# A float32 decoder trunk on one core: where three small pieces of work stand at the ends of its two mixers

## What is computed

```python
def reference(x, ffn_w_gate, ffn_w_up, ffn_w_down, norm_gain, ...):
    for i in range(DEPTH):                       # DEPTH = 2
        g = norm_gain[i]
        h = swiglu(rmsnorm(x, g[0]), ffn_w_gate[i, 0], ffn_w_up[i, 0], ffn_w_down[i, 0])
        x = x + MACARON_WEIGHT * rmsnorm(h, g[1])
        h = rmsnorm(x, g[2])
        j = i // N_MIXERS
        if i % N_MIXERS == 0:
            h = gla_mixer(h, gla_w_in[j], ..., gla_w_out[j])
        else:
            h = ssd_mixer(h, ssd_w_in[j], ..., ssd_w_out[j])
        x = x + rmsnorm(h, g[3])
        h = swiglu(rmsnorm(x, g[4]), ffn_w_gate[i, 1], ffn_w_up[i, 1], ffn_w_down[i, 1])
        x = x + MACARON_WEIGHT * rmsnorm(h, g[5])
    return x

def swiglu(h, w_gate, w_up, w_down):
    return (jax.nn.silu(h @ w_gate) * (h @ w_up)) @ w_down
```

## Time and profile before

| What | us |
|---|---|
| median of 3 runs | 1087.08 (1086.83 to 1087.44) |
| the profiled execution | 1086.96 |
| its span | 1085.2 |
| PE busy | 1075.1 |
| DVE busy | 787.6 |
| ACT busy | 652.8 |
| POOL busy | 87.2 |

### The profile page before, as it was taken

The page is one execution under the profiler, slowest core; times in us unless marked ns, Lnnn a source line. Parts: engine busy times, 40 slices in busy tenths (PEclk is TensorE's granted clock), DMA queues, the critical chain, the costliest instruction groups (busy, mean ns, idle before and its releaser), DMA issues.

```text
span 1085.2 us, 17549 instructions
## 1 busy us (share of the span) xinstructions
PE 1075.1 (99%) x6399; PEld 940.1 (87%) x6399; DVE 787.6 (73%) x1122; ACT 652.8 (60%) x1002; POOL 87.2 (8%) x138
## 2 busy tenths in 40 slices
PE   9999999999999999999999999999999999999997
PEld 7888888899888888888888888899999988888886
DVE  5867667785677666667766767889888888776664
ACT  7645446784676445458454447697777797454453
POOL 3000000011010000000000000153222211000000
PEclk9999999999999999999999999999999999999999
DMA  9864655375357555474655554595555536655531
GB/s 283 296 230 156 206 180 145 107 241 183 121 163 245 193 190 197 155 233 140 232 192 193 177 171 121 173 289 184 187 155 155 170 121 213 238 171 195 196 112 40
DMA packets 162881, 199.30 MB, mean 184 GB/s; under 512 B 6372, under 2 KB 145856, under 8 KB 162832
## 3 DMA queue, kind: packets, MB, share of 16 engines
q1 hardware_dynamic: 160288, 190.86, 53.9%
q0 software_dynamic: 2384, 7.72, 2.1%
q10 hardware_dynamic: 160, 0.08, 0.0%
HBM read 197.56 MB, written 1.08 MB: 183 GB/s over the span
## 4 chain that ended last, share of the span: by engine, by line
PE 92%; ACT 3%; DMA 2%; DVE 2%; issue 1%; SPq 0%; POOL 0%; DVEq 0%; ACTq 0%; POOLq 0%
PE ps L1772 27%; PE ps L1934 24%; PE ps L1948 13%; PE ps L1826 9%; PE ps L1835 6%; PE ps L1738 5%; PE ps L1859 4%; DMA raw<-in_ffn_w_up 1%; PE ps L1798 1%; PE ps L2294 1%; PE ps L2153 0%; ACT exps L882 0%; PE ps L2298 0%; DVE xres L1179 0%; PE ps L1757 0%
## 5 line engine op out<-in xcount | busy, mean ns | idle before, releaser
L1224 DVE TENSOR_TENSOR ws<-raw,ws 128x1024 fp32r<-128x1024 f32 x180 | 213.3, 1222 | 139.7 <-ACT ws L685 139.7
L1772 PE MATMUL ps<-ws,hT 128*128 128x512 f32 x1320 | 314.0, 392 | 0.0
L685 ACT ACTIVATE ws<-raw 128x1024 fp32r<-128x1024 f32 x183 | 184.7, 1053 | 173.2 <-PE ps L1948 160.3
L1772 PEld LDWEIGHTS ps<-ws,hT 128*128 128x128 f32 x1320 | 243.7, 188 | 49.5 <-issue 1.1
L1934 PE MATMUL ps<-xT,ws 128*128 128x512 f32 x1152 | 267.3, 389 | 0.2 <-ACT ws L685 0.2
L1934 PEld LDWEIGHTS ps<-xT,ws 128*128 128x128 f32 x1152 | 216.1, 188 | 45.5 <-ACT ws L685 0.6
L1146 DVE TENSOR_TENSOR ws<-raw,ws 128x2048 fp32r<-128x2048 f32 (+1 forms) x88 | 197.2, 2243 | 27.8 <-ACT ws L599 27.8
L599 ACT ACTIVATE ws<-raw 128x2048 fp32r<-128x2048 f32 x83 | 157.6, 1909 | 2.6 <-PE ps L1772 2.6
L1948 PEld LDWEIGHTS ps<-xT,ws 128*128 128x128 f32 x1152 | 142.6, 192 | 2.5
L1948 PE MATMUL ps<-xT,ws 128*128 128x256 f32 x1152 | 144.1, 283 | 0.0
L1826 PE MATMUL ps<-xT,ws 128*128 128x256 f32 x960 | 119.2, 284 | 0.0
(11 more groups left out here) (263 smaller groups left out, 864.3 us busy)
## 6 DMA issues: line engine op xcount, KB each, us to landing
raw<-in_ffn_w_down SPq DMA_DIRECT2D x88, 512.0 KB, 4.8
raw<-in_ffn_w_gate SPq DMA_DIRECT2D x86, 512.0 KB, 4.0
raw<-in_ffn_w_up SPq DMA_DIRECT2D x86, 512.0 KB, 5.0
raw<-in_ssd_w_in SPq DMA_DIRECT2D x48, 512.0 KB, 4.7
raw<-in_gla_w_in SPq DMA_DIRECT2D x24, 512.0 KB, 4.8
raw<-in_ssd_w_out SPq DMA_DIRECT2D x16, 512.0 KB, 4.3
raw<-in_gla_w_out SPq DMA_DIRECT2D x8, 512.0 KB, 5.5
exps<-cs_rows POOLq DMA_DIRECT2D x8, 512.0 KB, 5.1
```

Of the source, the lines that this page charges most:

```text
L685: act.activation(ws[:, 0:2, 0, c], raw[:, 0:2, c], ACT.Copy).then_inc(gu_hi, 1)
L1224: dve.tensor_tensor(ws[:, 0:2, 1, c], raw[:, 0:2, c], ws[:, 0:2, 0, c].bitcast(F32), ALU.subtract).then_inc(gu_lo, 1)
L1772: mm = pe.matmul(ps[:, 2 * t + n, :], hT[:, par, j, a, t * P:(t + 1) * P], ws[:, slot, b, off:off + 512], start=(first and j + a + b == 0) ...
```

## The change

Three edits.

1. In the SSD mixer's body `ahead` DVE writes the whole low part of the output weights of group n-2 (128x2048) at once, ahead of `norm`, where before it wrote the first half. The second half, which stood in the body `tail` between `wm` and the copy of the state, is gone from there.
2. At the ends of both mixers each of POOL's two low parts of 128x2x512 elements is made by four instructions of 128x2x128. The semaphore is still raised once for each 128x2x512.
3. At the boundary behind both mixers ACT writes the high parts of blocks 0 and 1 of x's first 128 tokens ahead of the last `post_square` (t = 1, second half), and the other six behind it.

```diff
@@ -554,9 +554,12 @@
                     pool.wait_ge(gu_hi, unit * NQ + NQ)
                     pool.wait_ge(x_ready, 4 * (b - 1) + 2)
                     pool.wait_ge(gu_lo, unit * NQ + NQ - 2)
-                    for c in (slice((NQ - 2) * QW, (NQ - 1) * QW), slice((NQ - 1) * QW, NQ * QW)):
-                        pool.tensor_tensor(ws[:, 0:2, 1, c], raw[:, 0:2, c], ws[:, 0:2, 0, c].bitcast(F32),
-                                           op=ALU.subtract).then_inc(gu_lo, 1)
+                    for q in range(NQ - 2, NQ):
+                        for o in range(0, QW, QW // 4):
+                            c = slice(q * QW + o, q * QW + o + QW // 4)
+                            ins = pool.tensor_tensor(ws[:, 0:2, 1, c], raw[:, 0:2, c], ws[:, 0:2, 0, c].bitcast(F32),
+                                                     op=ALU.subtract)
+                        ins.then_inc(gu_lo, 1)
                 if b > 0:
                     pool.wait_ge(post_read, 4 * b)
                     pool.dma_start(gpost[:, :], gain_row(2 * b + 1)).then_inc(gpost_in, 16)
@@ -756,9 +759,10 @@
                 post_square(b, 1, 0)
                 after_mixer = b < NPH and PHASES[b - 1][0] != "ffn"
                 if after_mixer:
+                    x_high(b, 0, range(2))
                     post_square(b, 1, 1)
                 if b < NPH:
-                    x_high(b, 0, range(KD // 2))
+                    x_high(b, 0, range(2 if after_mixer else 0, KD // 2))
                 if not after_mixer:
                     post_square(b, 1, 1)
                     post_root(b, 1)
@@ -1605,8 +1609,6 @@
                                 lo(SLOT_P3, g + n0[SLOT_P3])
                                 x_convolved(state_copied)
                             else:
-                                if tail:
-                                    lo_half(*out_unit(n - 2, n, n0), 1)
                                 state_copied()
                             if tail:
                                 transposed(C)
@@ -1682,7 +1684,7 @@
                     if first and ssd:
                         norm(g, tail)
                     if ssd and ahead:
-                        lo_half(*out_unit(g - 1, n, n0), 0)
+                        lo(*out_unit(g - 1, n, n0))
                     if ssd and tail:
                         lo_half(*out_unit(n - 1, n, n0), 0)
                     if scan and not (first and ssd) and not second:
```

## The result

| What | before | changed |
|---|---|---|
| median of 22 runs, us | 1087.08 (1086.80 to 1087.57) | 1088.45 (1088.09 to 1089.58) |
| span of the profiled execution | 1085.2 | 1086.8 |
| DVE busy, us and instructions | 787.6, 1122 | 789.2, 1121 |
| POOL busy, us and instructions | 87.2, 138 | 89.5, 150 |

The changed kernel takes 1.0013 times the time of before (95% interval 1.0007 to 1.0019): 1.37 us more, a small difference that is clear of the noise, and inside the 0.2% that the prediction calls no change. The forecast was 1087.6, in a range of 1086.1 to 1088.6.

What follows compares the result with a forecast made beforehand. The prediction took PE's row of matmuls (92% of the chain) to bound the kernel. Its terms, +0.4 for edit 1, +0.1 behind GLA and 0 behind SSD, made +0.5 us on 1087.08, so 1087.6, range 1086.1 to 1088.6.

Steps and rivals of the forecast that it cites:

- the ceiling: PE's waits at the mixers' ends, together 1.7 us or 0.16% of the time: the most the change could bring.
- the list of rivals: Its no-queue case at the SSD norm: one-input L1523 and L1528 pass POOL; total -0.2 us, 1086.9, chance 0.30.
- the case with one held step: SSD mixer's norm, edit 1: POOL holds one of L1529 to L1531; L1542 +0.35, saved 0.32 cancelled, 0 or -0.1.
- A quarter of 256 elements should take 0.62 to 0.66, like L525: POOL's low parts at both mixers' ends: eight quarters take 5.0 to 5.2 for 4.75, POOL ending 0.3 to 0.4 later.
- the rival of costly quarters: Both boundaries: quarters of 0.72 or more hold both x-update halves, 0.6 a boundary; total +1.7, 1088.8, chance 0.15.
- The bookkeeping of holds: DVE at both boundaries: L1151 waits for one POOL quarter, L1152 for the next, so L1151's saving is spent.
- may find POOL idle: DVE's L1179 at both boundaries: starts 308.67 and 899.06 before, POOL's last quarter ending at 308.8 and 899.1.
- So the 0.26 that PE gains behind GLA is lost 5 us later: Edit 3: PE's earlier first high part is offset by the later x update; +0.1 behind GLA, 0 behind SSD.
- the prediction's own sign: Check in the changed profile: forecast wrong if a POOL quarter takes over 0.7, or L1529 to L1531 take 0.16 each.

Runs made afterwards that it cites:

- edits 1 and 3 freed of their holds: Edits 1 and 3, POOL's last two dx products after `wm`, one-input Newton steps at t = 1 behind both mixers, against the kernel before: 1085.96 against 1086.93.
- dx later: Edit 1 alone with POOL's last two side products (dx, L525) issued only after DVE's `wm`, against the kernel before: 1086.72 against 1086.98, ratio 0.9999.

## Why the prediction came out as it did

- **What bounds the kernel, and the ceiling.** Right: PE carries the chain before and after, no kernel left the 0.2%, and the one with the lowest median, edits 1 and 3 freed of their holds, gains 0.97 of the 1.7 us that the prediction gave as the ceiling.
- **Edit 1**, forecast +0.4, measured +0.28 in the changed kernel and +0.31 alone. Each step came as worked out: L517 at 2.53, three steps held, and, counted from L517's start, L1542 0.86 later (4.73 for 3.87; forecast 0.9), L2294 0.86 later (6.60 for 5.74) and L2298, free of its wait, 0.48 later (7.69 for 7.21; forecast 0.5 to 0.6). Of these 0.48 PE had 0.20 back by its transposes behind SSD, a little more than the prediction allowed. What it didn't name is where PE first waits for the held steps: 0.56 at the transposes of y. Two details were wrong without harm to the sum. L1523 didn't pass POOL freely, as the list of rivals has it (see below). And the case with one held step was priced at +0.35 for L1542 and 0 or -0.1 for PE, as if none had been held before; but L1530 had been. With one held step and dx later, L1542 came 0.11 later (3.98 for 3.87) and PE gained 0.34.
- **Edit 2: the mis-sized term.** The step that failed is "A quarter of 256 elements should take 0.62 to 0.66, like L525": it took 0.742, eight took 5.62 in place of 5.0 to 5.2, and POOL ended 0.87 later than before in place of 0.3 to 0.4. L525 wasn't a like row: it has the same count but other operands, and no fp32r output. The like row was L558 itself, but one size of it can't show a fixed part. Rows 4 had a hint of one, though: 512 elements took 1.04 in one instruction (L520) and 1.20 in two (L525), 0.16 for one more instruction. Six more at that price, an estimate from these rows, make 4.75 + 0.96 = 5.71, close to the 5.62. The prediction had set 0.7 as the mark above which its forecast is wrong, and 0.72 for the rival of costly quarters, and the boundaries went that rival's way: +0.66 and +0.42 where the forecast had +0.1 and 0 and the rival about 0.6 on top of each. The bookkeeping of holds was half right. Both Newton steps took a hold, as in the forecast, but of both halves of the x update only one was held, behind SSD; behind GLA the update waited for POOL's last end instead.
- **The x update** "may find POOL idle": so it was behind GLA (309.45 against POOL's end at 309.40). Counted from POOL's start it still came 0.68 later than before (5.67 for 4.99), since POOL's end was 0.87 later, less the 0.19 by which L1179 had followed that end before.
- **Edit 3.** "So the 0.26 that PE gains behind GLA is lost 5 us later" is right for the edit alone (+0.02), by the hold that ends with POOL. With quarters it cost a further 0.27 behind GLA, which the prediction, with its quarters at a lower price, did not have. PE started its 22 matmuls there without a wait, as forecast.
- **Sum.** The time, 1088.45, lies 0.85 above the forecast and inside the range. The range held because it took in most of the costly quarters, to which 0.15 was given. So the number came out inside the range with the boundaries mis-sized, nearer to the rival's 1088.8 than to the forecast, and by the prediction's own sign (a quarter over 0.7) the forecast was wrong. More than 0.15 was due to that rival, by the hint in rows 4.

## What to carry to other kernels

Cutting an instruction into pieces to let another engine in paid each piece's fixed part here, and let in about one waiting instruction per piece: the chain of small steps then paid for two or three of its links, where the undivided instruction made it pay once in all. Take a piece's duration from two sizes of the same instruction; where there is only one size, at least add what one more instruction costs elsewhere on that engine. And look first whether the small steps can be brought into a form that isn't held, only at those places where they are, or whether the other engine's row has work that nobody wants yet.

## What the runs showed of the hardware

- **Who comes next when both have work.** In most places seen, a DVE step with two tensor inputs waited for the end of the POOL instruction that ran and went in ahead of the next one: 0.57, 0.54, 0.54 for three steps of 0.16 beside three POOL instructions, and 0.73, 0.66 for steps of 0.22 and 0.16 beside quarters. Steps issued 0.23 and 0.27 before a quarter's end went in behind it (0.25 and 0.29). But there are places that don't fit. With edit 2 alone, behind SSD, L1154 was issued at 897.89, before the fifth quarter ended (898.00) and before the sixth began. Yet it took 0.83, to the end of the sixth. POOL's two quarters, each from a timeline of its own:

```profile
897.26 0.74 POOL L560 TENSOR_TENSOR ws<-raw,ws 128x256 fp32r<-128x256 f32 x1
...
897.96 0.75 POOL L560 TENSOR_TENSOR ws<-raw,ws 128x256 fp32r<-128x256 f32 x1
```

  And L1529 of the kernel before, issued 0.01 ahead of an L525, wasn't held at all (0.16). So strict alternation isn't shown, and neither is how early a step has to be issued.
- **POOL's price.** 256 elements a partition, float32 to fp32r, took 0.742, four times as many about 2.39. A line through the two gives, as an estimate, a fixed part of 0.19 and 0.55 per 256 elements. Back to back, they overlapped by 0.04 each.
- **A form that isn't held, and from which size it is.** A 1-element step with a per-partition scalar for its second operand took 0.27 with POOL running, the same as in its other places. The one with two tensor inputs took up to 1.35. The Trainium skill, page "SBUF — State Buffer", section "Who interferes with whom", has it that a DVE instruction with at most one SBUF input outside the 2-port modes doesn't contend with GpSimd, and the 1-element rows agree. But one tensor input isn't enough. L1452, also a tensor-scalar, but on 256 elements, was held to 1.15. The norm's first step, L1523 (L1527 in the changed kernel), is a tensor-scalar on 2 elements with one tensor input. It took 0.16 with POOL idle, 0.22 in the kernel before beside L520, and 0.29 in the changed kernel beside L517 (before, then changed):

```profile
884.70 0.16 DVE L1523 TENSOR_SCALAR sm<-sm 128x2 f32<-128x2 f32 x1
```
```profile
876.47 0.29 DVE L1527 TENSOR_SCALAR sm<-sm 128x2 f32<-128x2 f32 x1 [0.21 <-ACT scr L968]
```

  It was issued 2.27 behind L517's start in both kernels, and it ended 0.02 to 0.03 behind the end of the POOL instruction in both, as the held steps do. So it reads as held too, from 2 elements on. The Trainium skill, page "SBUF — State Buffer", section "Who interferes with whom", says that a tensor-scalar can enter a 2-port mode and can then contend, and these two rows agree. No run here changed the size alone.
- **It holds both ways.** DVE's low part stretched POOL's L517, which takes 0.62 in other bodies, to 2.53, and DVE's x update stretched POOL's eight quarters from 5.62 to 6.51.
- **Open.** No run has the quarters with another number of pieces (two, say), so the point from which they would pay isn't known. The three two-input steps of the norm were never written in a one-input form, so what that would give edit 1 isn't known either.
